# Seven products in place of eight: the query and key projections of both layers and the last two channel blocks of layer 0

## The reference

```python
ssd_c, diff_c, mla_c = jnp.split(h_ctx @ w_in, cuts, axis=-1)
ssd_l, diff_l, mla_l = jnp.split(h_lat @ w_in, cuts, axis=-1)
# scan: the x, B and C channels of h @ w_in, 768 in all
xbc = jax.nn.silu(centred_dwconv(xbc, conv_w, conv_b))
# differential attention: queries and keys, 256 columns each
q, k, v = jnp.split(p, 3, axis=-1)
rp = lambda t: rope_2d(t, rows, cols)   # rotary embedding, latent tokens only
```

## Time and profile before

| | |
|---|---|
| time, median of 3 runs | 2095.87 us (2094.13 to 2097.17) |
| profiled execution: device time, span | 2094.3 us, 2092.2 us |
| busy in the span: PE, DVE, ACT, POOL | 1942.3, 721.6, 519.1, 186.9 us |
| mean granted clock of TensorE | 0.988 |
| layer 0: query/key projection, values | 41.5 to 108.9 us |
| layer 0: channel blocks | 305.6 to 366.6 us |
| layer 1: query/key projection, values | 1165.9 to 1203.2 us |

### The profile page before, as it was taken

The page is one execution under the profiler, slowest core; times in us unless marked ns, Lnnn a source line. Parts: engine busy times, 40 slices in busy tenths (PEclk is TensorE's granted clock), DMA queues, the critical chain, the costliest instruction groups (busy, mean ns, idle before and its releaser), DMA issues. The chain is left out here.

```text
span 2092.2 us, 25952 instructions
## 1 busy us (share of the span) xinstructions
PE 1942.3 (93%) x10858; PEld 934.4 (45%) x10858; DVE 721.6 (34%) x1335; ACT 519.1 (25%) x1020; POOL 186.9 (9%) x216
## 2 busy tenths in 40 slices
PE   5998999989989999999999999999898998888886
PEld 2656565544433333333334866655445333232222
DVE  2258565372431110111113476563624111111113
ACT  4146552452300000000003255524321100000012
POOL 1300000120011111212012000001100000000000
PEclk9999999999999999999999999999999999999999
DMA  9520304222289999999999223024419999999996
GB/s 351 147 81 1 141 1 152 90 105 96 82 343 401 393 399 395 394 401 393 402 395 301 111 82 141 1 90 153 165 61 357 395 408 408 408 409 409 409 409 261
DMA packets 164805, 530.64 MB, mean 254 GB/s; under 512 B 11016, under 2 KB 19538, under 8 KB 164690
## 3 DMA queue, kind: packets, MB, share of 16 engines
q1 hardware_dynamic: 149344, 489.49, 60.0%
q0 software_dynamic: 15120, 39.43, 6.1%
q10 hardware_dynamic: 226, 0.07, 0.0%
HBM read 507.98 MB, written 20.97 MB: 253 GB/s over the span
## 5 line engine op out<-in xcount | busy, mean ns | idle before, releaser
L3267 PE MATMUL ps<-ring,arena 128*64 128x512 f32 x1040 | 233.2, 597 | 13.6 <-DMA ring<-in_w_up 8.8
L3267 PE MATMUL ps<-arena 128*64 128x512 f32 x720 | 165.0, 604 | 3.6 <-DMA arena<-in_w_gate 3.2
L3267 PEld LDWEIGHTS ps<-ring,arena 128*64 128x64 f32 x1040 | 72.1, 137 | 161.6 <-issue 141.3
L3093 PE MATMUL ps<-ring,arena 128*128 128x512 f32 x320 | 141.6, 597 | 1.0 <-ACT arena L1442 0.6
L2366 DVE TENSOR_TENSOR arena<-arena,ps 128x512 f32<-128x512 f32 x32 | 22.0, 688 | 280.1 <-ACT arena L1487 280.1
L3316 PE MATMUL ps<-ring,arena 128*64 128x512 f32 x496 | 112.4, 596 | 5.8 <-DMA ring<-in_w_down 5.8
L2476 PE MATMUL ps<-arena,ring 128*128 128x256 f32 (+1 forms) x384 | 110.4, 447 | 2.5 <-DMA ring<-in_w_in 2.5
L1487 ACT ACTIVATE arena<-ps 128x512 f32<-128x512 f32 x32 | 19.1, 597 | 373.4 <-PE ps L3267 373.4
L3316 PE MATMUL ps<-arena 128*64 128x512 f32 x432 | 97.9, 595 | 5.2 <-DMA arena<-in_w_down 4.5
L1066 ACT ACTIVATE arena<-ps 128x768 f32<-128x768 f32 (+6 forms) x111 | 79.9, 724 | 88.0 <-PE ps L2494 45.3
L3267 PEld LDWEIGHTS ps<-arena 128*64 128x64 f32 x720 | 50.4, 139 | 107.0 <-issue 100.3
(11 more groups left out here) (417 smaller groups left out, 2821.8 us busy)
## 6 DMA issues: line engine op xcount, KB each, us to landing
ring<-in_w_up SPq DMA_DIRECT2D x33, 2048.0 KB, 14.7
ring<-in_w_gate SPq DMA_DIRECT2D x32, 2048.0 KB, 21.1
ring<-in_w_down SPq DMA_DIRECT2D x30, 2048.0 KB, 23.0
ring<-in_ada_w SPq DMA_DIRECT2D x24, 2048.0 KB, 9.9
arena<-in_w_down SPq DMA_DIRECT2D x19, 2048.0 KB, 23.2
arena<-in_w_gate SPq DMA_DIRECT2D x18, 2048.0 KB, 22.5
arena<-in_w_up SPq DMA_DIRECT2D x12, 2048.0 KB, 13.6
ring<-in_w_in SPq DMA_DIRECT2D x6, 2048.0 KB, 14.0
```

Of the source, the lines that this page charges most:

```text
L3093: ins = mm(o[:, hf * 512:(hf + 1) * 512], mix, wo[hf][:, k, :], start=k == 0, stop=k == KD - 1)
L3267: ins = mm(px[0][hf * 64:hf * 64 + 64, col:col + 512], xl[e % 2][:, at:at + CAP_L], w[c][:, hf * 512:hf * 512 + 512], start=b + c == 0, st ...
```

## The change

The blocks of queries and keys are made as two pairs, (0, 2) and (1, 3), by the scheme of the channel blocks: fourteen groups of four matmuls, each over half the tokens (384 in layer 0, 256 in layer 1) and half the inputs, in place of sixteen. A pair p uses the tiles of `qk`+2p and `qk`+2p+1. VectorE makes eight sums first (L1742 in the new file: four of tokens, four of weights) and combines the products; ScalarE copies each pair's first product out and later scales the queries in place. The blocks end together, so they are turned and embedded in the order 2, 0, 3, 1; blocks 3 and 1 are turned behind the first value product.

In layer 0 alone, channel blocks 4 and 5 become such a pair too. Its weight sums stand within the step of block 3, and the order becomes 2, 0, 3, 1, 5, 4. The job table is as it was.

```diff
-        CONV_ORDER = (2, 0, 3, 1, 4, 5)
+        CM += [CM[0], CM[2]]
+        CONV_ORDER = ((2, 0, 3, 1, 5, 4), (2, 0, 3, 1, 4, 5))
...
+        def last_pair_of_channels(x):
+
+            return SW[1 + x // 2][:, :, P * (x % 2):P * (x % 2) + P]
...
+                    if l == 0 and m == 1:
+                        act.wait_ge(S["half_products"], products0 + 11)
+                        act.activation(E1[0], J.tile(conv_job(l, 4))[:, 0:HT], ACT.Copy).then_inc(S["half_out"], 1)
...
+                qk_sum(TQ[0], qk_rows(0, 1), qk_rows(0, 0), ALU.subtract)
+                qk_sums_done(1)
+                qk_sum(TQ[1], qk_rows(4, 1), TQ[0], ALU.subtract)
+                dve.wait_ge(ring_full[n4 % RING], ring_turns(n4) * 16)
+                qk_sum(SQ[0], qk_weights(1, 0), qk_weights(1, 4))
+                qk_sums_done(3)
+                qk_sum(SQ[1], SQ[0], qk_weights(0, 0), ALU.subtract)
+                qk_sum(SQ[2], qk_weights(0, 0), qk_weights(1, 0), ALU.subtract)
+                qk_sum(TQ[2], qk_rows(4, 1), qk_rows(0, 1), ALU.subtract)
+                qk_sums_done(4)
+                qk_sum(SQ[3], qk_weights(0, 4), SQ[1], ALU.subtract)
+                qk_sum(TQ[3], qk_rows(4, 0), TQ[1], ALU.subtract)
...
+                for p in range(2):
+                    dve.wait_ge(S["half_products"], products0 + 5 + p)
+                    qk_sum(EQ[p], EQ[p], qk_tile(p, 0, 1))
+                for p in range(2):
+                    qk_sums_done(11 + p)
+                    dve.wait_ge(*J.filled(jb("qk") + 2 * p))
+                    TT(UQ[p], EQ[p], qk_tile(p, 0, 1), ALU.add).then_inc(*J.free(jb("qk") + 2 * p))
...
+                def qk_late(p):
+
+                    dve.wait_ge(*J.freed(jb("qk") + 2 * p))
+                    dve.wait_ge(S["half_products"], products0 + 7 + 2 * p)
+                    qk_sum(qk_out(2 + p, 1), UQ[p], qk_tile(p, 1, 0))
+                    qk_sum(EQ[p], EQ[p], qk_tile(p, 1, 0))
+
+                def qk_early(p):
+
+                    dve.wait_ge(S["half_products"], products0 + 8 + 2 * p)
+                    qk_sum(qk_out(2 + p, 0), UQ[p], qk_tile(p, 1, 1))
+
+                def qk_last(p):
+
+                    qk_sums_done((14, 17)[p])
+                    dve.wait_ge(*J.filled(jb("qk") + 2 * p + 1))
+                    TT(qk_out(p, 1), EQ[p], qk_tile(p, 1, 0), ALU.add).then_inc(*J.free(jb("qk") + 2 * p + 1))
+
+                qk_late(0)
+                qk_early(0)
+                qk_last(0)
+                qk_late(1)
+                for i, m in enumerate((2, 0, 3, 1)):
+                    if i == 1:
+                        qk_early(1)
+                        qk_last(1)
+                    dve.wait_ge(*qk_ready(l, m))
...
-                for m in CONV_ORDER:
+                def bc_weight_sums():
...
+                    wb15, s_ = ringv(n15), [last_pair_of_channels(x) for x in range(4)]
+                    dve.wait_ge(*J.filled(conv_job(l, 2)))
+                    half_sum(s_[0], wb15[:, 0:4, P:2 * P], wb15[:, 4:8, P:2 * P], ALU.add)
+                    sums_done(21)
+                    half_sum(s_[1], s_[0], wb15[:, 0:4, 0:P], ALU.subtract)
...
+                    half_sum(s_[2], wb15[:, 0:4, 0:P], wb15[:, 0:4, P:2 * P], ALU.subtract)
+                    half_sum(s_[3], wb15[:, 4:8, 0:P], s_[1], ALU.subtract)
...
+                def bc_halves():
+
+                    j0, j1 = conv_job(l, 4), conv_job(l, 5)
+                    dve.wait_ge(S["half_out"], out0 + 3)
+                    dve.wait_ge(S["half_products"], products0 + 12)
+                    half_sum(CM[4][:, 0:HT], E1[0], J.tile(j0)[:, 0:HT], ALU.add)
+                    dve.wait_ge(S["half_products"], products0 + 13)
+                    half_sum(E1[0], E1[0], J.tile(j0)[:, 512:512 + HT], ALU.add)
+                    sums_done(28)
...
+                    TT(U3[0], E1[0], J.tile(j0)[:, 512:512 + HT], ALU.add).then_inc(*J.free(j0))
+                    dve.wait_ge(*J.freed(j0))
+                    half_sum(CM[5][:, HT:TOK], U3[0], J.tile(j1)[:, 0:HT], ALU.add)
+                    half_sum(E1[0], E1[0], J.tile(j1)[:, 0:HT], ALU.add)
+                    dve.wait_ge(S["half_products"], products0 + 15)
+                    half_sum(CM[5][:, 0:HT], U3[0], J.tile(j1)[:, 512:512 + HT], ALU.add)
+                    sums_done(30)
+                    dve.wait_ge(*J.filled(j1))
+                    TT(CM[4][:, HT:TOK], E1[0], J.tile(j1)[:, 0:HT], ALU.add).then_inc(*J.free(j1))
...
+                for m in CONV_ORDER[l]:
                     j = conv_job(l, m)
                     if m == 0:
                         late_half(1)
                     if m == 3:
                         early_half(1)
+                        if l == 0:
+                            bc_weight_sums()
                         last_half(1)
+                    if m == 5 and l == 0:
+                        bc_halves()
...
-                    pe.wait_ge(*J.freed(jb("qk") + m))
+                    pe.wait_ge(*qk_ready(l, m))
...
-                for m in range(4):
-                    feature_major(jb("qk") + m, w, m * P, P, t0,
-                                  ready=(latents_ready if l else first_h) if m == 0 else None)
-                    if m:
-                        quarter_turned(m - 1)
...
+                for p in range(2):
+                    pe.wait_ge(*J.empty(jb("qk") + 2 * p))
+                    qk_product(p, 0, 0, qk_weight(p, 0, 0), qk_rows(0, 0), 0 if p == 0 else None).then_inc(S["half_products"], 1)
+                for p in range(2):
+                    pe.wait_ge(S["half_out"], out0 + p + 1)
+                    qk_product(p, 0, 0, qk_weight(p, 0, 4), qk_rows(4, 0), 4 if p == 0 else None).then_inc(S["half_products"], 1)
+                pe.wait_ge(S["half_sums"], sums0 + 4)
+                for p in range(2):
+                    qk_product(p, 0, 1, of_qk_pair(1, p), TQ[1]).then_inc(S["half_products"], 1)
+                for p in range(2):
+                    pe.wait_ge(S["half_sums"], sums0 + 11 + p)
+                    qk_product(p, 0, 1, of_qk_pair(2, p), TQ[2]).then_inc(*J.fill(jb("qk") + 2 * p))
+                for p in range(2):
+                    pe.wait_ge(*J.empty(jb("qk") + 2 * p + 1))
+                    qk_product(p, 1, 0, of_qk_pair(0, p), TQ[0]).then_inc(S["half_products"], 1)
+                    if p:
+                        quarter_turned(2)
+                    qk_product(p, 1, 1, qk_weight(p, 1, 4), TQ[3]).then_inc(S["half_products"], 1)
+                    pe.wait_ge(S["half_sums"], sums0 + (14, 17)[p])
+                    qk_product(p, 1, 0, of_qk_pair(3, p), qk_rows(4, 1)).then_inc(*J.fill(jb("qk") + 2 * p + 1))
+                quarter_turned(0)
                 w = arrived(wb + 5)
                 wv = w
                 if l:
                     token_major(jb("v"), w[:, :, 0:256], range(CT, CT + 2), 256, 256)
                     quarter_turned(3)
+                    quarter_turned(1)
                     pe.wait_ge(*J.freed(jb("kc")))
                     pe.wait_ge(*J.freed(jb("vc")))
                 else:
                     token_major(jb("v"), w[:, :, 0:256], range(0, 4), 256, 256)
                     quarter_turned(3)
+                    quarter_turned(1)
                     token_major(jb("v") + 1, w[:, :, 0:256], range(4, 6), 256, 256)
...
-                pe.wait_ge(*w_.next(S["qk_roped"], 3))
+                pe.wait_ge(*w_.next(S["qk_roped"], 2))
...
-                feature_major(conv_job(l, 4), w, 0, P)
-                block_rows(l, 2, 2)
-                feature_major(conv_job(l, 5), w, P, P, conv_start(l, 5) // P)
...
+                    pe.wait_ge(*J.empty(conv_job(l, 4)))
+                    bc_product(0, 0, w[:, 0:4, 0:P], rows_half(0, 0)).then_inc(S["half_products"], 1)
+                    block_rows(l, 2, 2)
+                    pe.wait_ge(S["half_out"], out0 + 3)
+                    bc_product(0, 0, w[:, 4:8, 0:P], rows_half(4, 0)).then_inc(S["half_products"], 1)
+                    pe.wait_ge(S["half_sums"], sums0 + 24)
+                    bc_product(0, 1, last_pair_of_channels(1), TH[1]).then_inc(S["half_products"], 1)
+                    pe.wait_ge(*J.empty(conv_job(l, 5)))
+                    bc_product(1, 0, last_pair_of_channels(0), TH[0]).then_inc(S["half_products"], 1)
+                    pe.wait_ge(S["half_sums"], sums0 + 28)
+                    bc_product(0, 1, last_pair_of_channels(2), TH[2]).then_inc(*J.fill(conv_job(l, 4)))
+                    bc_product(1, 1, w[:, 4:8, P:2 * P], TH[3]).then_inc(S["half_products"], 1)
+                    pe.wait_ge(S["half_sums"], sums0 + 30)
+                    bc_product(1, 0, last_pair_of_channels(3), rows_half(4, 1)).then_inc(*J.fill(conv_job(l, 5)))
```

(26 more changed lines are left out.)

102 lines of the change are left out of this document (78 added, 24 removed).

## The result

The changed kernel takes 2125.75 us (median of 4 runs, 2122.62 to 2130.03) against 2095.6 us before: a ratio of 1.0145, interval 1.0122 to 1.0168, or 30 us slower. The forecast was 2119 in 2105 to 2127; two of the four runs (2128.27 and 2130.03) lie above that range. The profiled execution took 2122.62 us with a span of 2120.5, 28.3 longer than before's.

What follows compares the result with a forecast made beforehand. TensorE's matmuls were taken to bound the changed places. Net waits of 17.1 us plus 6.4 of half clock made 23.5 on the profiled 2094.3, 2117.8; as a median 2119, range 2105 to 2127.

Steps and rivals of the forecast that it cites:

- The saving: Fewer matmul groups in both layers' queries and keys and layer 0's channel blocks: 5.2 + 3.5 + 2.6 = 11.3 us.
- A: Layer 0 queries and keys: second values wait 4.2 us for block 1's sines; net 0.6 us later.
- B: Layer 0 channel blocks 4 and 5: TensorE idles 7.7 and 5.4 us for row additions; net 10.5 us later.
- C: Layer 1 queries and keys: waits of 0.2, 2.5, 2.1 and 4.3 us; net 6.0 us later.
- The rule on banks: Skill page against the change: rotate independent groups through PSUM banks; keeping the old order would spare A and C 8.5.
- From place to end: A shift of TensorE at the changed places passes through the experts to the end one for one.
- The step that was too small: the clock: Half clock for 3.2 us behind each of four long gaps, costing 1.6 each, 6.4 us in all.
- worse: Rival: slow clock also stretches groups VectorE waits for, or 6.5 us drops follow several gaps; above 2127, chance 0.06.
- Waits without the clock: Rival: the idle waits cost 17.1 us with no drop of the clock; 2113, chance 0.08.
- Only the channel blocks stall less: Rival: row 1 freed at once, so the channel blocks wait less; 2110, or 2105 with fewer drops; chance 0.10.
- no net change: Rival: A wins what C loses and B costs nothing; within 4 us of 2096, chance 0.08.
- do what it says: Rival: VectorE frees each tile before TensorE comes, so 11.3 us are won; 2084.6, chance 0.06.

Runs made afterwards that it cites:

- gaps_filled: The changed kernel plus small matmuls that nobody reads in TensorE's four long gaps, 16 to 31 per gap; 2114.5 us, 1.0099 of before.
- rows_early: The changed kernel with layer 0's channel blocks reordered: weight-sum product earlier, row block behind four products, row 2 added among combinations; 2117.04 us, 1.0096 of before.
- turns_early: The changed kernel with the turns of blocks 3 and 1 inside (layer 0) or ahead of (layer 1) the first value product; 2114.08 us, 1.0090 of before.
- only_bc: The kernel before with only layer 0's channel blocks 4 and 5 by seven products, queries and keys plain; 2111.52 us, 1.0074 of before.
- bc_mended: only_bc with ScalarE's first-product copy, the row block, row additions and cumulative-sum copies reordered; 2094.51 us, 0.9995 of before.
- layer0_mended: bc_mended plus layer 0's queries and keys by seven products, block 0 turned and embedded earlier, turns as in turns_early; layer 1 plain; 2096.37 us, 0.9998 of before.

## Why the prediction was right

**The saving and the waits.** Each idle bracket was there, at the tile and behind the instruction that the prediction named: 4.07 (forecast 4.2) and 1.16 (1.3) in A, 7.36 (7.7) and 5.21 (5.4) in B, 0.19 (0.2), 1.81 (2.5; the two times that the prediction subtracts there give 2.7), 1.85 (2.1) and 4.28 (4.3) in C. The net of A, B and C without the clock was forecast at 0.6, 10.5 and 6.0, together 17.1, and measured in gaps_filled as 0.6, 10.2 and 5.5, together 16.3. One wait was not foreseen, 0.51 at 57.73: the first groups did not run at half clock this time (10.59 for 32 records) and TensorE came earlier. In gaps_filled they did (12.28), and the wait is not there. That the loss sits in the tiles' order is shown by rows_early and turns_early, which took the named gaps away without any change of arithmetic.

**The rule on banks.** turns_early puts the turns back among other matmuls, and A loses its 4.07 and C all but 0.75 of its 4.28, and 1.2 of the 1.85 ahead of the values: near the price that the prediction set beside the Trainium skill's "Perfetto Trace Analysis", section "Matmuls" (independent groups should rotate through PSUM banks), 8.5.

**From place to end.** The shift of TensorE reaches the issues of the experts and the end, as said: only_bc's delay lies in layer 0 alone and is all in its time. That it passes one for one can't be read to the microsecond, since the clock changes it on the way: in the changed kernel 25.1 behind place C became 28.2 at the issues, in gaps_filled 22.2 became 16.8 at the end.

**The step that was too small: the clock.** The prediction took 6.4, a stretch of 3.2 us behind each of the four long gaps. Right behind them the rows show 1.6 + (1.6 + 1.2) + (1.6 + 0.8) + 1.4 = 8.2 lost, as two of the stretches were longer. More came where nothing was changed: 3.1 us in 487.90 to 494.30, behind a gap of 1.91 that before has in the same length at full clock,

```profile
470.00:494.00 24.00, 22.81 (x68) 11.27 (x69) 5.29 (x5) 4.92 (x14) 1.96 (x4) 1.00 0.44 178
```

(the row is of the kernel before), and 5.2 in the scan of layer 1 where before loses 3.2. By the clock loss of the runs the changed kernel lost 41.4 against 25.1, and filling the four gaps gave some 10 us back. So the forecast of 23.5 was 6.6 us short, and short on the clock: the waits came out 0.8 smaller than forecast. That the result lies within the range is in part luck: it is 1.3 us under the upper end, two of four runs are above it, and what the rival *worse* asked for nearly came, slow stretches of over 3.2 us behind two of the gaps (0.50 and 0.61 behind 7.36, 0.50 and 0.74 behind 5.21). The section of the Trainium skill that was weighed ("TensorE: Matmul & The Clock Gate", section "HAM oscillation — how this bites in real kernels") speaks of long waits, and the four long gaps agree with it. It does not cover the shorter ones, and there the rows are mixed: behind 1.16, 1.81 and 1.85 the clock stayed at 1.00, a gap of 2.02 in rows_early was followed by 0.57 (360.00 to 363.40), and of 2.13 to 2.78 in before three of four were followed by half clock.

**The rivals.** *Waits without the clock* (2113) is refuted by the half clock behind the four gaps and by what filling them gave back. *Only the channel blocks stall less* and *no net change* are refuted by the brackets. *Worse* is not far off, as said. That the change could do what it says is true of layer 0 with another order of VectorE's work (bc_mended's 1.5 at the gate projection, layer0_mended's 6 to 8 at the clock of before), not as it was written, and not in layer 1. No version without fillers is clearly faster than before (bc_mended 0.9995, layer0_mended 0.9998).

## What to carry to other kernels

When a tiled kernel does fewer matmuls, ask for each tile what stood between its filling and its next use, and whether that cover is still there: results that end together leave their consumers in a row at the end, and the next user of the tile waits for the last. Put the release of a tile (the reading instruction) ahead of work that only SBUF needs, and put the tile's next use behind other matmuls. Price a new gap of some microseconds in TensorE with more than its length, and read the mean clock of every run beside its time before believing a difference under 1%.
